# A mixture-of-experts stage: down weights split on ScalarE and GpSimd, down projection as three split products

## The reference, cut to what matters

```python
N_EXPERTS, EXPERT_FF, MOE_BLOCK = 32, 256, 128
def expert_block(args):
    xb, e = args                                   # xb: 128 rows of tokens, e: the expert
    hb = jax.nn.silu(xb @ w_gate[e]) * (xb @ w_up[e])
    return hb @ w_down[e]                          # 128 x 256 by 256 x 1024: the down projection
```

## Time and profile before

| | |
|---|---|
| time of the kernel, median of 3 runs | 2547.04 us (2540.92 to 2551.4) |
| the profiled execution, first to last instruction | 2556.9 us |
| TensorE matmul busy in the whole span | 2192.0 us (86%) |
| VectorE, ScalarE, GpSimd busy | 1307.4, 1055.8, 551.0 us |
| the expert loop, first to last weight split | 879.9 to 1216.6 us |
| in it, 907 to 1233 us: TensorE, VectorE, ScalarE, GpSimd busy | 322.25, 217.42, 178.10, 82.71 us of 326 |
| granted TensorE clock in it (1.00 is full) | 1.00 |
| DMA engines busy in it | 0.86, 327 GB/s |

### The profile page before, as it was taken

How to read it: one execution, slowest core, us unless ns; L and a number is a source line. 1 busy time by engine, 2 the same in 40 slices (tenths; PEclk the granted TensorE clock), 3 DMA queues, 4 the chain that set the end, 5 groups by cost and what they waited for, 6 DMA issues and landing times. The chain is left out here.

```text
span 2556.9 us, 34124 instructions
## 1 busy us (share of the span) xinstructions
PE 2192.0 (86%) x12244; PEld 1813.6 (71%) x12244; DVE 1307.4 (51%) x2177; ACT 1055.8 (41%) x1924; POOL 551.0 (22%) x587
## 2 busy tenths in 40 slices
PE   6996897999887499999489999688869799965778
PEld 5885886999876366666268888578758687855657
DVE  3343675555454466766352120667655353428853
ACT  3332555555342155555252120256544233327741
POOL 1003100622011121322120000456521000016821
PEclk9998898999998599999689999889979899987889
DMA  4686866422063479998464221433162424142152
GB/s 155 198 247 178 241 207 162 128 64 62 21 217 118 173 303 370 361 341 333 151 228 147 83 80 49 124 78 76 36 232 100 157 93 150 62 137 70 43 190 91
DMA packets 216868, 399.73 MB, mean 156 GB/s; under 512 B 90528, under 2 KB 111392, under 8 KB 204048
## 3 DMA queue, kind: packets, MB, share of 16 engines
q1 hardware_dynamic: 177152, 315.04, 38.8%
q10 hardware_dynamic: 28384, 61.62, 6.4%
q0 software_dynamic: 11184, 21.13, 2.3%
HBM read 300.68 MB, written 114.85 MB: 163 GB/s over the span
## 5 line engine op out<-in xcount | busy, mean ns | idle before, releaser
L78 PE MATMUL pe_acc<-pe_w,hT 128*128 128x512 f32 x960 | 226.7, 398 | 5.3 <-DVE hT L721 5.3
L78 PEld LDWEIGHTS pe_acc<-pe_w,hT 128*128 128x128 f32 x960 | 184.6, 193 | 44.5 <-DVE hT L721 5.7
L78 PE MATMUL ex_gu<-hT,ex_xT 128*128 128x512 f32 x792 | 194.8, 402 | 0.8 <-DVE hT L2386 0.8
L2386 DVE TENSOR_TENSOR hT<-ex_raw,hT 128x2048 fp32r<-128x2048 f32 x66 | 150.9, 2287 | 84.0 <-ACT hT L2357 84.0
L78 PE MATMUL pg_acc<-hT,pg_w 128*128 128x512 f32 x768 | 180.3, 396 | 8.7 <-DVE pg_w L263 8.7
L78 PEld LDWEIGHTS pg_acc<-hT,pg_w 128*128 128x128 f32 x768 | 145.7, 190 | 42.4 <-DVE pg_w L263 9.1
L78 PEld LDWEIGHTS ex_gu<-hT,ex_xT 128*128 128x128 f32 x792 | 147.7, 190 | 34.6 <-DVE hT L2386 1.2
L2357 ACT ACTIVATE hT<-ex_raw 128x2048 fp32r<-128x2048 f32 x66 | 126.3, 1915 | 38.5 <-PEq L47 23.9
L302 DVE COPY pe_o<-pe_acc 128x512 f32<-128x512 f32 x28 | 19.3, 691 | 206.5 <-PE pe_acc L78 206.4
L1762 PE MATMUL ab_op<-ab_v,ab_pT 128*128 128x64 f32 x1024 | 121.3, 272 | 0.0
L2315 PE MATMUL ex_dn<-ex_wd,ex_hT 128*128 128x512 f32 x264 | 118.7, 592 | 0.8 <-ACT ex_hT L2351 0.8
(11 more groups left out here) (496 smaller groups left out, 5084.5 us busy)
## 6 DMA issues: line engine op xcount, KB each, us to landing
ex_raw<-in_w_gate SPq DMA_DIRECT2D x33, 1024.0 KB, 7.3
ex_raw<-in_w_up SPq DMA_DIRECT2D x33, 1024.0 KB, 11.4
ex_wd<-in_w_down SPq DMA_DIRECT2D x33, 1024.0 KB, 12.3
pe_raw<-in_even_w_in SPq DMA_DIRECT2D x6, 2048.0 KB, 8.9
pg_raw<-in_odd_w_in SPq DMA_DIRECT2D x5, 2048.0 KB, 9.1
scr_q<-pa_o SPq DMA_DIRECT2D x32, 256.0 KB, 4.1
scr_k<-pa_o SPq DMA_DIRECT2D x32, 256.0 KB, 3.7
hT<-scr_k SPq DMA_DIRECT2D x16, 512.0 KB, 6.8
```

The source lines that it names most:

```text
L78: mm = pe.matmul(out, a(p, k), b(q, k), start=(k == 0 and i == 0), stop=(k == n - 1 and i == 2))
L2386: dve.tensor_tensor(split(s, LO)[:, :, g, :], raw[:, s % NW, g, :].rearrange("p (k n) -> p k n", k=8), split(s, HI)[:, :, g, :].bitcast(F3 ...
```

## The change

- Only two `wd` buffers instead of four (ND = 2), and the load of down weights waits on `wd_lo` instead of `dn_ok`. Only the loads of two blocks are started ahead of the stage instead of three.
- ScalarE rounds the down weights of block s into a new tile `wdh` (a copy of 128 x 2048, two buffers). It stands behind the up half and ahead of the sigmoid of block s-1. It waits for the weights, and from s = 2 on for `dn_ok` to reach s-1, which is the down projection of block s-2, since that reads the same buffer.
- GpSimd subtracts (128 x 2048) into `wdl`. It stands between the gather of block s and the scatter of block s-4.
- VectorE gets one more subtraction (128 x 256) for the lo part of the turned hidden rows, at the head of its iteration.
- TensorE's down projection becomes two calls of `product` with two slices each, 12 fp32r matmuls of 128 x 512 instead of the 4 of float32, and waits on `wd_lo` instead of the load.

```diff
-NW, ND, NX = 3, 4, 3
+NW, ND, NX = 3, 2, 3
...
-                for e in range(NW):
+                for e in range(ND):
                     weights.load(sp, slice(e, e + 1), e)
...
-    def load(self, sp, e, b):
+    def load(self, sp, e, b, wd_lo=None):
...
+        if wd_lo is not None:
+            sp.wait_ge(wd_lo, b - ND + 1)
         sp.dma_start(self.wd[:, b % ND, :], self.w_down[:, e, :]).then_inc(self.wd_in[b % ND], 16)
...
-                for b in range(NW, BLOCKS):
-                    sp.wait_ge(w_lo, 2 * (b - NW + 1))
-                    if b >= ND:
-                        sp.wait_ge(dn_ok, b - ND + 1)
+                for b in range(ND, BLOCKS):
+                    if b >= NW:
+                        sp.wait_ge(w_lo, 2 * (b - NW + 1))
...
+                    b = s - 1
+                    if 0 <= b < BLOCKS:
+                        pool.wait_ge(wd_hi, b + 1)
+                        if b >= 2:
+                            pool.wait_ge(dn_ok, b - 1)
+                        pool.tensor_tensor(wdl[:, b % 2, :], wd[:, b % ND, :], wdh[:, b % 2, :].bitcast(F32),
+                                           ALU.subtract).then_inc(wd_lo, 1)
+                        pool.wait_ge(wd_lo, b + 1)
...
-                        pe.wait_ge(wd_in[b % ND], 16 * (b // ND + 1))
+                        pe.wait_ge(wd_lo, b + 1)
                         pe.wait_ge(hT_ok, b + 1)
...
                         for n in range(2):
-                            for k in range(2):
-                                mm = pe.matmul(dn[:, n * BANK:(n + 1) * BANK], hTs[:, b % 2, k, :],
-                                               wd[:, b % ND, k * D + n * BANK:k * D + (n + 1) * BANK], start=(k == 0), stop=(k == 1))
+                            mm = product(pe, dn[:, n * BANK:(n + 1) * BANK], 2, lambda p, k: hTs[:, b % 2, p, k, :],
+                                         lambda q, k: down[q][:, k * D + n * BANK:k * D + (n + 1) * BANK])
                         mm.then_inc(dn_ok, 1)
...
+                        act.wait_ge(wd_in[s % ND], 16 * (s // ND + 1))
+                        if s >= 2:
+                            act.wait_ge(dn_ok, s - 1)
+                        act.activation(wdh[:, s % 2, :], wd[:, s % ND, :], ACT.Copy).then_inc(wd_hi, 1)
                     b = s - 1
                     if 0 <= b < BLOCKS:
                         act.wait_ge(gu_ok, b + 1)
...
+                    b = s - 2
+                    if b >= 0:
+                        dve.wait_ge(hT_hi, b + 1)
+                        dve.tensor_tensor(hTs[:, b % 2, LO, :, :].rearrange("p k n -> p (k n)"), tph[:, 0:2 * P],
+                                          hTs[:, b % 2, HI, :, :].rearrange("p k n -> p (k n)").bitcast(F32),
+                                          ALU.subtract).then_inc(hT_ok, 1)
```

More of the change, by code:

```diff
@@ L2199, in experts @@
         h2 = st.sb("ex_h2", [P, 2, FF])
-        hTs = st.sb("ex_hT", [P, 2, 2, P])
+        hTs = st.sb("ex_hT", [P, 2, 2, 2, P], F32R)
+        wdh, wdl = (st.sb("ex_" + n, [P, 2, 2 * D], F32R) for n in ("wdh", "wdl"))
         ob = st.sb("ex_ob", [P, 2, D])
@@ L2209, in experts @@
                                         "hturned", "hT_ok", "dn_ok", "ob_a", "ob_b"))
+        hT_hi, wd_hi, wd_lo = (st.sem("ex_" + n) for n in ("hT_hi", "wd_hi", "wd_lo"))
         stored = [st.sem(f"ex_stored{s}") for s in range(2)]
@@ L2213, in experts @@
                                         "hT_ok", "dn_ok", "ob_ok", "stored", "free", "passed"))
-        f_gug, f_hTs = gu[0], hTs[:, 0, :, :]
+        f_gug, f_hTs = gu[0], xg[:, 1, 0:2 * P].rearrange("p (k n) -> p k n", k=2)
         f_xTs = ob[:, 1, :].rearrange("p (k n) -> p k n", k=8)
@@ L2233, in _ @@
                         e = bass.ds(sp.value_load(over[0:1, 0:1], min_val=0, max_val=NE - 1), 1)
-                    weights.load(sp, e, b)
+                    weights.load(sp, e, b, wd_lo)
                 def body(j):
@@ L2312, in _ @@
                             pe.wait_ge(ob_b, b)
+                        down = wdh[:, b % 2, :], wdl[:, b % 2, :]
                         for n in range(2):
-                            for k in range(2):
-                                mm = pe.matmul(dn[:, n * BANK:(n + 1) * BANK], hTs[:, b % 2, k, :],
-                                               wd[:, b % ND, k * D + n * BANK:k * D + (n + 1) * BANK], start=(k == 0), stop=(k == 1))
+                            mm = product(pe, dn[:, n * BANK:(n + 1) * BANK], 2, lambda p, k: hTs[:, b % 2, p, k, :],
+                                         lambda q, k: down[q][:, k * D + n * BANK:k * D + (n + 1) * BANK])
                         mm.then_inc(dn_ok, 1)
@@ L2350, in _ @@
                             act.wait_ge(dn_ok, b - 1)
-                        act.activation(hTs[:, b % 2, :, :].rearrange("p k n -> p (k n)"), tph[:, 0:2 * P], ACT.Copy).then_inc(hT_ok, 1)
+                        act.activation(hTs[:, b % 2, HI, :, :].rearrange("p k n -> p (k n)"), tph[:, 0:2 * P], ACT.Copy).then_inc(hT_hi, 1)
                     if s < BLOCKS:
```

## The result

The change makes the kernel slower: 2717.12 us (2713.65 to 2723.24) against 2549.22 (2540.92 to 2559.67), a ratio of 1.0654 [1.0628, 1.0679]. The forecast was 2684 with a range up to 2712.

The account below looks back on a forecast made before the run. TensorE was taken to bound the kernel before, at 10.30 us an iteration; a ring of 13.01 plus 1.62 for the clock made 14.63. Thirty iterations (+130), start +2, next iteration +4.5 and tail +1 gave 2684 us, range 2632 to 2712.

Parts of the forecast that it names:

- The direction: Whole kernel: slower with chance 0.97, same 0.01, faster 0.02.
- the ring: Expert loop: down matmuls, rounding, sigmoid, gated product and next iteration's TensorE work wait for each other, 13.01 us an iteration.
- The late gather: GpSimd's gather of block s+1 behind the subtraction: rows landing just late for TensorE, 0.1 us; 1.4 if landing takes 7.7.
- the clock: TensorE after each pause: gate and up matmuls slowed to 7.33 us by a halved clock, 1.62 us more per iteration.
- the start: Before the first hidden rows: two more roundings on ScalarE, +2 us.
- The pause of 3.47 us: TensorE idle each iteration between down matmuls and turning of hidden rows: 0.20 + 1.92 + 1.35 us.
- ScalarE's wait ahead of the rounding: Each loop iteration: ScalarE waits some 4 us before rounding down weights, released by the down matmuls.
- The rival that the gather binds on top: Expert loop: gathers land late, adding half the lateness; 15.2 to 16.0 us an iteration, 2701 to 2727 us, chance 0.17.
- GpSimd's subtraction: Down weights' lo part on GpSimd, 128 x 2048: 4.72 us, hidden in the loop, cost 0.
- The shorter down projection: TensorE: twelve fp32r matmuls in 2.84 us against 3.43 for float32, 0.59 us less per block.
- the exclusion as pace: Expert loop: VectorE and GpSimd operations that block each other follow in turn, 11.4 us an iteration, 2583 us, chance 0.02.
- The faster case: Expert loop: the rounding never waits for the down projection, TensorE stays the bound at 9.54 us, 2524 us, chance 0.02.

Follow-up runs that it names:

- a3: Changed kernel with the gather of block s+1 ahead of GpSimd's subtraction and twelve unused matmuls behind each down projection: 2647.54 us, ratio 1.0377.
- a1: Changed kernel with GpSimd's gather of block s+1 written ahead of the subtraction of block s-1: 2699.9 us, ratio 1.0594.
- b1: Changed kernel with GpSimd's subtraction cut from 2048 to 64 columns, TensorE taking the hi tile for the lo tile: 2694.48 us, ratio 1.0568.
- c2: Changed kernel, down weights rounded and loaded one step later, gathers two blocks ahead, scatter of s-3 ahead of subtraction, VectorE doing half of it: 2541.72 us, ratio 0.9957.
- c1: Changed kernel, down weights rounded and loaded one step later, gathers two blocks ahead, scatter of block s-3 ahead of GpSimd's whole subtraction: 2576.67 us, ratio 1.0098.
- a4: Changed kernel with ScalarE's sigmoid of block s-1 ahead of the rounding of down weights: 2709.91 us, ratio 1.0624.

## Why the prediction was wrong

The direction and the ring were right, and a3 isolates the ring. The step that failed is the price of what comes on top of it. The late gather was put at 0.1 and left out of the sum, the clock at 1.62 with the transposes at full speed, and the start at +2. The runs show 0.50, 1.93 and +9.4. All three were too low, and the time came 33 us above the forecast and 5 us above the range.

- **The ring**, 13.01 us by the sum of its pieces, is 12.90 in a3. Most of the difference is in the down matmuls, 2.74 us by starts (1062.88 to 1065.62) and not 2.84. The pause of 3.47 us is 3.42 by starts (1065.62 to 1069.04); the 3.25 of the profile's rows is counted from the modelled end of the last matmul. ScalarE's wait ahead of the rounding, forecast as some 4 us, is 6.2 on average (180.4 us in 29 waits), since transposes, gate and up take longer and gathers come late.
- **The clock**, 1.62 us, is 1.93 (1.84 by the means). I had noted that the transposes may run at half the clock too and taken them at full speed. They did run slow: 1.57 us instead of 0.79, and in a1 the gate and up matmuls took 6.74 us on average, by starts, against 5.67 in a3 behind its first iteration. I had 7.33 for these, so that part was too high by half a microsecond, and the part of the transposes, about 0.8, was missing. The Trainium skill, "TensorE: Matmul & The Clock Gate", "What's actually happening", has the slow clock as the default; the trace agrees as far as it goes, with 0.50 in the window at 1063 us, right behind a pause.
- **The gather.** This step failed most in the loop. I took the fast end of the old landings, cost 0.1, because DMA would be less busy, and left even that out of the 14.63. DMA is indeed at 0.62, but a gather still takes 9.3 us from issue to landing, 3.0 of them writing: 6.3 us behind it, where 4.95 were free. TensorE waited for it in 12 of 29 iterations, up to 1.3 us, and a1 puts the price at 0.50 an iteration. The rival that the gather binds on top (15.2 to 16.0 us, 2701 to 2727) holds 15.33 and 2717, so it was the case that came, with 0.17 against 0.59. That its number fits so well is partly luck: its formula, half the lateness, gives 0.68 where 0.50 was measured, and the clock made up the rest.
- **The start**, +2, is +9.4 from the stage's first rounding (+8.0 by the profiles' own times). I had worked out the exclusion of the two engines for the full loop, where it is hidden, and priced the start by ScalarE's roundings alone. There nothing hides it: VectorE's first weight subtraction of block 1 took 5.28 us, the second 6.52, and the hidden rows waited. b1 shows 6.2 us of it. The other 3.2 us go with the first gather, which landed 3.6 us later; the forecast had no term for that, and put the loads at 0. The roundings that it did price cost nothing there (b1).
- **GpSimd's subtraction**, estimated at 4.72 us, is 4.54. It cost nothing by itself in the loop, as I had said and b1 shows; VectorE's stretched operation was 2.61 us (1065.90).
- **The shorter down projection**, forecast as 0.59 us, is worth 0.69 by starts (2.74 in a3 against 3.43 before). The first iteration of c2, in which TensorE never waits, is 9.49 us against 10.13, 0.64 less.

Together: -0.11 for the ring, +0.31 for the clock, +0.50 for the gather make 15.33 out of 14.63, 21 us over thirty iterations, and the start 7 more, some 28 of the 33 us. Of the other 5, 2.2 lie with the kernel before, whose median was 2547.04 when I forecast and 2549.22 with a fourth run; the rest was not isolated.

Of the rivals, the exclusion as pace (11.4 us) was rightly called hidden here, and it is what bounds c1 (11.02) once ScalarE's wait is gone. I had written that I found no way to that: rounding one iteration later is one. The faster case (9.54 us) is nearly reached by c2 (9.79), and it shows how little there was to win: 0.64 us of 10.13, against 4.5 us of work on GpSimd and 1.9 on ScalarE that must find room.

Not settled: what sets at which point of the slow stretch the clock comes back (gate and up took between 6.0 and 7.5 us). More than two buffers of down weights or of their rounded copies were not tried with the changed kernel, nor were loads of three blocks ahead of the stage.

## What to carry to other kernels

A wait for a buffer that is put into an engine's queue holds everything behind it: before inserting one, look up who needs the next instruction of that queue, and place the new one behind it or for a block whose buffer is long free. Opening one ring only pays down to the next, so what stands behind the same wait, here the gather and the scatter, has to be moved in the same step (a4 won 7 us, a4 with the two transfers moved 107). A stall in a loop of matmuls has to be priced at both clocks, and with all that TensorE does behind it, transposes too. Price the start of a loop by itself: what the full loop hides may be bare there, and fewer loads ahead of it put new ones beside the first gather.

## What the runs showed of the hardware beyond expectation

VectorE and GpSimd hold each other up. A subtraction of GpSimd stretched one of VectorE to nearly three times its length: 128 x 2048 took 6.52 us behind GpSimd's 4.50 us one, and 2.28 where that was tiny. In the other direction a VectorE subtraction held GpSimd's writing of a gather, 3.02 us (1069.70) instead of 1.02. The Trainium skill, "SBUF — State Buffer", "Who interferes with whom", calls the ports that the two engines share "an exclusive lock". The two rows at the start agree: the VectorE operation ends 2.2 us after GpSimd's (906.34 to 908.51), about its whole length alone.

Indirect transfers stay slow at a lower load: gathers land 9.3 us after their issue (median) at a DMA share of 0.62, against 10.7 at 0.82. Of the 9.3, some 3.0 are GpSimd's writing; of the 10.7, mostly 1.0.

Idle time of 3.25 us costs about 5.2 us here: itself, and 1.93 us for the slow clock behind it. Twelve matmuls that nobody uses, 2.96 us of work, gave these 1.93 us back in every iteration, where no gather was late (a1 against a3).
